# A two-layer encoder kernel: a layer's small parameters arrive as one ready-made block, and one instruction clears the semaphores

## The reference, cut to what matters

```python
for l in range(DEPTH):                                   # DEPTH = 2
    h = rms_norm(x, norm_mix[l])
    proj = h @ w_in[l]                                   # 2048 x 4096
    pa, pb, pq, pk, pv, rr, rk, rv, rz = jnp.split(proj, SPLIT_POINTS, axis=-1)
    ya = fourier_mix(pa, fourier_w[l])
    yb = s5_mix(pb, s5_lam_re[l], s5_lam_im[l], s5_log_step[l], ...)
    yc = attention_mix(pq, pk, pv, attn_q_norm[l], attn_k_norm[l], cos, sin)
    yd = rwkv7_mix(rr, rk, rv, rz, rwkv_mu[l], rwkv_w0[l], ...)
    ycat = rms_norm(stack(ya, yb, yc, yd), branch_norm[l])
    x = x + ycat @ w_out[l]
    x = x + peer_ffn(rms_norm(x, norm_ffn[l]), peer_w_query[l], peer_sub_keys[l],
                     peer_u[l], peer_v[l])               # 16384 experts, top 16 of each of 8 heads
```

## Time and profile before

| | us |
|---|---|
| three runs | 4009.41, 4014.94, 4017.21 |
| median | 4014.94 |
| the profiled execution, its own time | 4015.24 |
| its span, first to last instruction | 4013.4 |
| PE busy | 3753.4 (94%) |
| DVE busy | 2291.9 (57%) |
| ACT busy | 429.4 (11%) |
| POOL busy | 964.7 (24%) |
| mean granted clock of TensorE | 0.974 of full speed |

### The profile page before, as it was taken

The page is one execution under the profiler, slowest core; times in us unless marked ns, Lnnn a source line. Parts: engine busy times, 40 slices in busy tenths (PEclk is TensorE's granted clock), DMA queues, the critical chain, the costliest instruction groups (busy, mean ns, idle before and its releaser), DMA issues. The chain is left out here.

```text
span 4013.4 us, 63920 instructions
## 1 busy us (share of the span) xinstructions
PE 3753.4 (94%) x26660; PEld 3401.8 (85%) x26660; DVE 2291.9 (57%) x4099; ACT 429.4 (11%) x1020; POOL 964.7 (24%) x868
## 2 busy tenths in 40 slices
PE   6997889999999999999879978899999999999997
PEld 5786774899999999999767867748999999999997
DVE  5965742785287544443469657517853875444434
ACT  1022210100111000000010232101001110000000
POOL 2610000034033333333225100000341333333331
PEclk9997899999999999999989978999999999999999
DMA  5430015399799999999744300154997999999997
GB/s 156 136 116 10 2 43 162 126 372 401 290 384 382 415 415 415 414 413 414 305 133 130 116 10 1 43 162 142 379 404 288 382 385 415 415 415 415 413 413 302
DMA packets 334770, 1077.47 MB, mean 268 GB/s; under 512 B 52196, under 2 KB 150872, under 8 KB 268440
## 3 DMA queue, kind: packets, MB, share of 16 engines
q1 hardware_dynamic: 223896, 670.72, 44.0%
q0 software_dynamic: 110592, 402.70, 25.3%
HBM read 1071.23 MB, written 2.10 MB: 267 GB/s over the span
## 5 line engine op out<-in xcount | busy, mean ns | idle before, releaser
L1747 PE MATMUL bank<-ex_W,ex_tile 128*128 128x160 f32 x8192 | 1132.3, 300 | 38.8 <-DMA ex_tile<-in_peer_v 38.8
L1747 PEld LDWEIGHTS bank<-ex_W,ex_tile 128*128 128x128 f32 x8192 | 1114.9, 190 | 59.7 <-DMA ex_tile<-in_peer_v 53.0
L1674 PE MATMUL bank<-ycT,ex_tile 128*128 128x160 f32 x8192 | 1140.2, 300 | 20.3 <-DMA ex_tile<-in_peer_uT 19.9
L1674 PEld LDWEIGHTS bank<-ycT,ex_tile 128*128 128x128 f32 x8192 | 1116.9, 190 | 36.0 <-DMA ex_tile<-in_peer_uT 30.4
L1631 POOL DMA_INDIRECT ex_row<-in_peer_u,ex_rows x384 | 403.5, 1051 | 1852.7 <-DVE ex_rows L1907 1187.4
L1943 DVE SCALAR_TENSOR_TENSOR ex_sums<-ex_row,ex_weight,ex_sums 128x2048 f32<-128x2048 f32 x186 | 436.9, 2349 | 412.9 <-DMA ex_row<-in_peer_v,ex_rows 412.8
L1937 DVE CUSTOM_DVE_ANT_0 ex_row<-ex_row,ex_h_wide 128x2048 f32<-128x2048 f32 x192 | 438.5, 2290 | 363.7 <-DMA ex_row<-in_peer_u,ex_rows 362.4
L1631 POOL DMA_INDIRECT ex_row<-in_peer_v,ex_rows x384 | 363.7, 947 | 878.9 <-DVE ex_sums L1943 565.7
L359 PE MATMUL pj_bank<-pj_hT,pj_piece 128*128 128x256 f32 x2048 | 458.7, 383 | 5.6 <-DMA pj_piece<-in_w_in 3.8
L359 PEld LDWEIGHTS pj_bank<-pj_hT,pj_piece 128*128 128x128 f32 x2048 | 387.9, 191 | 71.5 <-issue 13.8
L826 PE MATMUL bank<-arena,ycT 128*128 128x512 f32 x512 | 222.4, 593 | 2.0 <-PEq L911 2.0
(11 more groups left out here) (375 smaller groups left out, 3107.0 us busy)
## 6 DMA issues: line engine op xcount, KB each, us to landing
ex_tile<-in_peer_uT SPq DMA_DIRECT2D x256, 1024.0 KB, 8.1
ex_tile<-in_peer_v SPq DMA_DIRECT2D x256, 1024.0 KB, 8.2
pj_piece<-in_w_in SPq DMA_DIRECT2D x32, 2048.0 KB, 8.8
arena<-in_w_out SPq DMA_DIRECT2D x16, 2048.0 KB, 8.1
query_w<-in_peer_w_query SPq DMA_DIRECT2D x16, 1024.0 KB, 5.8
ex_row<-in_peer_u,ex_rows POOLq DMA_INDIRECT x384, 13.0
ex_row<-in_peer_v,ex_rows POOLq DMA_INDIRECT x384, 12.4
x<-in_x SPq DMA_DIRECT2D x1, 2048.0 KB, 8.9
```

Source lines behind the costliest of these rows:

```text
L1674: mm = mmul(o, ring[:, j % SLOTS, k * P:k * P + P], hT[k // 4][:, k % 4, 0:DENSE], start=(k == 0), stop=(k == KT - 1))
L1747: mm = mmul(bank[:, at_, lo:lo + DENSE], ring[:, i % SLOTS, m * P:m * P + P], W[:, j, :], start=(j == 0 and m % 3 == 0), stop=(j == TILES ...
```

## The change

The small parameters are laid out on the host as they must stand in SBUF: a block `cols` of 128 partitions by 218 columns for each layer (122 columns that were `pcol`, 96 that were turned from `srow`), and a third block of zeros behind the last layer's. Three things follow.

- The block of layer 0 is loaded ahead of `x`. The block of the next layer is loaded in `experts`, between the last piece of `w_query` and the first tile of `peer_uT`. The semaphore `cols_in` is made ahead of the loop and is not cleared in it; it is waited for by count.
- In `mixers` the 17 loads, the spreading of the step sizes, the two transposes on PE and the copy to `pcol` are gone. `pcol` is a view of `cols`. The copy of 96 columns into `s5_v` reads `cols` and stands between DVE's two scalings.
- The semaphores of a lap have numbers in a row, and one instruction clears their range. Before there were 122 of them, now there are 119, since three are gone with the loads.

```diff
         consts = sb(whole, "consts", [P, where["eps_gn"][1]])
-        pcol = sb(whole, "pcol", [P, NROWS])
+        cols = sb(whole, "cols", [P, NROWS + 96])
+        pcol = cols[:, 0:NROWS]
...
                 sp.dma_start(consts[:], t["consts"]).then_inc(loaded, 16)
+                sp.dma_start(cols[:], t["cols"][0]).then_inc(cols_in, 16)
                 sp.dma_start(x[:], t["x"][0].rearrange("(b p) d -> p b d", p=P)).then_inc(loaded, 16)
...
                 def _(sp):
-                    for s in first_sem[kept:]:
-                        sp.sem_clear(s)
+                    numbers = [s.num for s in first_sem[kept:]]
+                    assert numbers == list(range(numbers[0], numbers[0] + len(numbers)))
+                    sp.sem_clear(range(numbers[0], numbers[-1] + 1))
...
                 sp.dma_start(out[0].rearrange("(b p) d -> p b d", p=P), x[:]).then_inc(stored, 16)
+                sp.wait_ge(cols_in, 16 * (DEPTH + 1))
                 sp.wait_ge(stored, 16)
...
             @block.sync
             def _(sp):
-                rows_load(sp, ROW_SRC)
-                for i, name in enumerate(("s5_lam_re", "s5_lam_im")):
-                    sp.dma_start(srow[32 * i:32 * i + 32, :],
-                                 t[name][layer].rearrange("d (g e) p -> (d g) (e p)", e=2)).then_inc(rows_in, 16)
-                sp.dma_start(ls2[64:96, :], t["s5_log_step"][layer].rearrange("d (g e) -> (d g) e", e=2))\
-                    .then_inc(rows_in, 16)
                 for n, u in enumerate(PIECES):
...
                 for b in range(TB):
-                    if b == 1:
-                        pe.wait_ge(rows_in, 17 * 16)
-                        tr(bank[:, 7, 0:NROWS], rows[0:NROWS, :], c("ident")[0:NROWS, 0:NROWS])
-                        pe.wait_ge(ls_ready, 1)
-                        tr(bank[:, 7, 256:352], srow[:, :], c("ident")[0:96, 0:96]).then_inc(rows_T, 1)
                     pe.wait_ge(h_ready, b + 1)
                     for k in range(KT):
-                        if b == 1 and k == 12:
-                            pe.wait_ge(cols_ready, 2)
...
                     if b == 0:
-                        dve.wait_ge(rows_in, 17 * 16)
-                        do(V.tensor_copy(srow[64:96, :].rearrange("q (e p) -> q e p", e=2),
-                                         ls2[64:96, :].unsqueeze(2).to_broadcast([32, 2, S5P])), ls_ready)
-                dve.wait_ge(rows_T, 1)
-                do(V.tensor_copy(pcol[:], bank[:, 7, 0:NROWS]), cols_ready)
-                do(V.tensor_copy(v[:, 0:3], bank[:, 7, 256:352].rearrange("p (a b) -> p a b", a=3)), cols_ready)
+                        dve.wait_ge(cols_in, layer * 16 + 16)
+                        do(V.tensor_copy(v[:, 0:3], cols[:, NROWS:NROWS + 96].rearrange("p (a b) -> p a b", a=3)), cols_ready)
...
                 for h in range(WRING, PEER_H):
                     sp.wait_ge(q_mm, h - WRING + 1)
                     query_piece(nc, t, layer, query, sp, h)
+                sp.dma_start(cols[:], t["cols"][layer + 1]).then_inc(cols_in, 16)
                 whole_laps = TILES // SLOTS
```

More of the change, by code:

```diff
@@ L152, in col @@
             return pcol[:, at:at + n]
-        loaded, base_set, stored = sem("loaded"), sem("base_set"), sem("stored")
+        loaded, base_set, stored, cols_in = sem("loaded"), sem("base_set"), sem("stored"), sem("cols_in")
         with nc.Block() as block:
@@ L177, in build @@
             mixT = sb(mix, "mixT", [P, 16, SEQ])
-            mixers(nc, t, layer, sem, sb, ps, c, col, x, pcol, mus, mixT, rwT, ycT)
+            mixers(nc, t, layer, sem, sb, ps, c, col, x, pcol, mus, mixT, rwT, ycT, cols, cols_in)
             mix.close()
@@ L195, in build @@
             route(nc, t, layer, sem, sb, bank, c, col, x, ycT, hT, query, out_w)
-            experts(nc, t, layer, sem, sb, bank, c, x, hT, query, W, low, layer_base, row_in)
+            experts(nc, t, layer, sem, sb, bank, c, x, hT, query, W, low, layer_base, row_in, cols, cols_in)
             rw.close()
@@ L218, with mixers @@
 EL = 16
-def mixers(nc, t, layer, sem, sb, ps, c, col, x, pcol, mus, mixT, rwT, ycT):
-    rows_in, piece_in = sem("pj_rows_in"), [sem(f"pj_piece_in{i}") for i in range(2)]
-    rows_T, cols_ready, tables_in = sem("pj_rows_T"), sem("pj_cols_ready"), sem("mix_tables_in")
+def mixers(nc, t, layer, sem, sb, ps, c, col, x, pcol, mus, mixT, rwT, ycT, cols, cols_in):
+    piece_in = [sem(f"pj_piece_in{i}") for i in range(2)]
+    cols_ready, tables_in = sem("pj_cols_ready"), sem("mix_tables_in")
     h_ready, hT_mm, hT_ready = sem("pj_h_ready"), sem("pj_hT_mm"), sem("pj_hT_ready")
     rms_ready, piece_mm, piece_out = sem("pj_rms"), sem("pj_mm"), sem("pj_out")
-    ls_ready, s5_act, s5_arg, pool_own = sem("pj_ls_ready"), sem("pj_s5_act"), sem("pj_s5_arg"), sem("pj_pool")
+    s5_act, s5_arg, pool_own = sem("pj_s5_act"), sem("pj_s5_arg"), sem("pj_pool")
     dve_own, act_own = sem("pj_dve"), sem("pj_act")
@@ L248, in mt @@
             return tables[:, lo if a is None else lo + a:hi if b is None else lo + b]
-        rows = sb(st, "pj_rows", [P, P])
-        srow = sb(st, "pj_srow", [96, P])
-        ls2 = sb(st, "pj_ls2", [96, 2])
         h = sb(st, "pj_h", [P, D])
@@ L1529, in served, with experts @@
     return BEFORE + max(j - FIRST + 1, 0) * 9 // 10
-def experts(nc, t, layer, sem, sb, bank, c, x, hT, query, W, low, layer_base, row_in):
+def experts(nc, t, layer, sem, sb, bank, c, x, hT, query, W, low, layer_base, row_in, cols, cols_in):
     q_mm, q_out, score_mm, score_out = [sem("ex_" + n) for n in ("q_mm", "q_out", "score_mm", "score_out")]
@@ L2020, with columns @@
         "branch_norm", "w_out", "norm_ffn", "peer_w_query", "peer_sub_keys", "peer_u", "peer_v"]
+_SMALL = ["norm_mix", "norm_ffn", "rwkv_mu", "rwkv_w0", "rwkv_a0", "rwkv_k_k", "rwkv_k_a", "rwkv_r_k", "rwkv_ln_w",
+          "rwkv_ln_b", "branch_norm", "s5_d", "attn_q_norm", "attn_k_norm", "s5_lam_re", "s5_lam_im", "s5_log_step"]
+def columns(inputs):
+    small = [np.asarray(inputs[n], np.float32) for n in _SMALL]
+    out = np.zeros((DEPTH + 1, P, NROWS + 96), np.float32)
+    for a in range(DEPTH):
+        rows = [s[a].reshape(-1, P) for s in small[:14]]
+        rows += [s[a].reshape(2 * S5G // 2, P) for s in small[14:16]]
+        rows += [np.repeat(small[16][a].reshape(2 * S5G // 2, 2), S5P, axis=1)]
+        out[a] = np.concatenate(rows, 0).T
+    return out
 def kernel(**inputs):
@@ L2027 @@
     nc = bacc.Bacc("TRN2", target_bir_lowering=False, num_devices=1)
-    arrays = {f"in_{n}": np.ascontiguousarray(inputs[n]) for n in _INS}
+    arrays = {f"in_{n}": np.ascontiguousarray(inputs[n]) for n in _INS if n not in _SMALL}
+    arrays["in_cols"] = columns(inputs)
     u = np.asarray(inputs["peer_u"]).reshape(DEPTH, TILES, KEYS, KT, P)
```

## The result

The changed kernel takes 3990.45 us (median of four runs, 3988.45 to 3992.34) beside 4016.07 us of the kernel before (four runs). The ratio is 0.9939, 95% interval 0.9921 to 0.9956. The forecast was 3991.0 us in a range of 3983.0 to 4000.5. On a second chip both were run again: 3990.95 against 4013.44 us, ratio 0.9947 (0.9931 to 0.9964). By the two ratios that is 25 and 21 us less.

The account below looks back on a forecast made before the run. PE in the sweeps was the largest item, untouched, so only PE's idle time outside them could pay. 14.7 + 1.2 + 4.6 + 1.7 + 2.4 - 0.4 = 24.2 us off 4015.2 gave 3991.0 us, range 3983 to 4000.5.

Parts of the forecast that it names:

- The clears: At both laps' ends, 121 of 122 semaphore clears go at 61 ns each, with nothing hiding them: 14.7 us.
- The copies: On DVE's way to hT at a lap's start, two copies leave the path: 0.61 us a lap, 1.2 us.
- The 17 loads: At a lap's start SP's queue frees earlier, matrices land sooner and PE's wait before L376 goes: 4.6 us together.
- L721: DVE instruction before PE's stall, thought to wait for POOL's L612; 2.40 us becomes 1.21, 2.4 us in both laps.
- The first load: Layer 0's cols load goes ahead of x at the kernel's start and delays it: cost 0.4 us, bounds 0 to 0.9.
- The clock in the second lap: PE's first 64 projection matmuls keep full clock as idle time ahead shrinks to about 3 us: 1.7 us.
- The jump back: From SP's drain at the lap's end to ACT's next start: 4.4 us, moving up behind the clears unchanged.
- only the clears pay: Rival: matrices land no earlier or PE finds another wait at L376; 15.5 us left, 3999.7 us, chance 0.14.
- slower: Rival: SP's tiles and POOL's gathered rows meet anew in the sweeps, near 4023 us; chance 0.02.
- The clock stays up: Rival: PE keeps 2.4 GHz through its shortened 6.6 us stall, some 6 us more gained, 3985 us; chance 0.13.

Follow-up runs that it names:

- Bringing the hold back alone: Changed kernel with 17 small loads, into a tile nobody reads, ahead of the pieces on SP's queue; 4009.84 against 4023.25 us for the kernel before, ratio 0.9971.
- POOL is pushed across: Changed kernel with one added wait, so POOL's first table runs across DVE's L692 to L697; 4009.72 against 4023.25 us for the kernel before, ratio 0.9966.
- the block alone: Changed kernel with its 119 semaphores cleared one by one; 4017.86 against 4023.25 us for the kernel before, on another chip 4002.14 against 4013.44 us.
- once the stall was gone: Changed kernel with two projection parts moved from PE's last unit to its first; 3974.12 against 4011.43 us for the kernel before, ratio 0.9906.

## Why the prediction was right

*The clears* (forecast 14.7 us). Right in mechanism and size: 7.2 us a lap by SP's drains, and the run with this part alone, 15 us, agrees. The long clear, priced like a single one, took 0.23 us.

*The copies* (1.2). L359's counterpart starts 16.51 us after ACT, before 17.13, 0.62 us in the first lap. The copy that moved lies in DVE's wait for PE, as said; that wait is now 2.72 us.

*The 17 loads* (4.6). Right in mechanism, and in size against the profile that the working used. DVE's L668 went from 40.69 to 33.72, forecast 33.7, and the wait for the turn is gone. Bringing the hold back alone brought the wait back. But 2.54 us is not what every first lap lost: in the second profile of the kernel before the slow clock covered that wait, and the two starts then gave 5.0 us where the sum has 7.55 with its terms for the copies, the loads and the clock.

*L721* (2.4). Right, and the cause shown: 1.21 and 1.20 us a lap, and 4.2 us lost a lap where POOL is pushed across. In the second pair of profiles the first lap gave 0.35 us, since L721 had waited less there.

*The first load* (-0.4). 0.3 us in the first profile, 0.7 in the second; in two other traces with the block ACT started 1.3 and 1.5 us later than before the change, so the price varies.

*The clock in the second lap* (1.7). This step failed, although its number appeared in the first profile. The working had PE's idle time shrink from 3.76 to about 3 us and took that as enough to keep 2.4 GHz. It isn't: at 2.94 us the clock dropped in 12 of 12 laps. In that profile the second batch of turns happened to take 3.35 and 3.67 us, and PE was idle for only 1.55 and 1.24 us. The usual lap of the changed kernel pays 1.7 us, in both laps, and in its second profile it did.

What made up for it was not in the sum. The store lands 6.4 us after its issue in all eleven traces with the block and 7.2 to 7.5 us in the three without it; why, isn't shown. The jump back, forecast at 4.4 us as before, took 3.8 us in the first profile of the changed kernel and between 2.9 and 3.8 in the others. Together that is 1.5 to 2.5 us. So the closeness of 3990.45 to 3991.0 is partly luck. The four mechanisms are not, though the sizes of two of them depend on how the clock happens to fall.

Of the rivals, "only the clears pay" is excluded by the block alone, which gives 10 us by itself (6 to 14), and "slower" by the time and by the sweeps, 1217 to 1219 us a lap in both profiles of both kernels. "The clock stays up" through the stall was wrong at 6.63 us (the stretch from 80 to 120 us has a mean clock of 0.87 after the change too), and right once the stall was gone.

## What to carry to other kernels

Time in which no engine is busy, at a loop's end, is worth reading instruction by instruction: here the 122 clears of each lap, which no busy column counts, cost some 15 us in both laps. When a queue's head is cleared, look at every wait that hung on it, also on other engines: two of the four gains, PE's first turn and L721, came at instructions that the edit doesn't touch. Before adding such gains up, profile the kernel twice: a slow clock can cover a wait in one execution and leave it bare in the next. And an edit that only shortens PE's idle time may leave the clock as slow as it was; work in the gap is what helps, such as parts moved into a stall.

## What the runs showed of the hardware

- Clearing a range of semaphores costs about 30 ns plus 1.7 ns for each; clearing them one by one costs 61 ns each.
- A multiplication on VectorE with both inputs in SBUF and one on GpSimd ran strictly one after the other: 1.2 us became up to 3.37 us on VectorE, and 1.93 and 2.35 us became 2.91 and 3.21 us on GpSimd. With one of its two inputs in PSUM VectorE wasn't held up: before the change L744 to L749 kept 0.7 us beside POOL's L607 and L608.
- The jump back to the loop's head took SP 4.5 and 4.6 us before and 0.9 us after, and 0.8 us with either of the two cuts in its program alone, while ACT still needed 2.9 to 3.8, against 4.4 and 4.6 before. The Trainium skill says that a taken branch waits for its target's instructions if they are no longer in the engine's small window of fetched ones (Runtime: NRT & Kernel Launch, "Instruction fetch mechanics"). A shorter SP program that still has its head at hand fits this, but no run here shows the fetches, and the length at which it changes wasn't looked for.
- Between the turns of `x` and the projection, idle times of PE of 2.50 to 3.76 us were followed by a clock of 1.2 GHz in all sixteen laps that have one (twelve of them with 2.94 us), at a price of 1.7 us in the twelve and up to 3.1 us; 1.85 us and less never were. At another place, ahead of the first turn, 2.54, 2.91 and 3.73 us left the clock at 2.4 GHz and 3.12 us did not, so the length alone is no rule.
